# Streaming the columns of a matmul in another order, in nine stages of a two-block transformer kernel

## What is computed

```python
def swiglu(h, w_gu, w_down):                      # D_FF = 2816
    g, u = jnp.split(h @ w_gu, 2, axis=-1)
    return (jax.nn.silu(g) * u) @ w_down
...
    for i in range(DEPTH):                        # two layers, 272 tokens
        f = swiglu(rms_norm(h, ln_ffn1[i, 0]), ffn1_w_gu[i], ffn1_w_down[i])
        h = h + 0.5 * rms_norm(f, ln_ffn1[i, 1])
        # i == 0: a short convolution between two projections; i == 1: differential attention
        h = h + rms_norm(m, ln_mix[i, 1])
        f = swiglu(rms_norm(h, ln_ffn2[i, 0]), ffn2_w_gu[i], ffn2_w_down[i])
        h = h + 0.5 * rms_norm(f, ln_ffn2[i, 1])
    return h[:, N_META:]                          # 256 tokens from here on
...
    merged = (sigmoid(gate_a) * (o_a @ w_br_dsa) + sigmoid(gate_b) * (o_b @ w_br_moba))
    x = x + gt_m * (merged @ w_out)
    ...
    x = x + gt_f * ((jax.nn.silu(g_ff) * u_ff) @ w_down)
```

## Time and profile before

| | |
|---|---|
| median of 3 runs | 1584.47 us (1582.22 to 1591.33) |
| the profiled execution's own time | 1585.17 us |
| its span, first to last instruction | 1583.4 us |
| TensorE busy with matmuls | 1499.4 us, 11846 matmuls |
| weight loads busy | 1471.8 us |
| VectorE, ScalarE busy | 1059.7 us, 684.2 us |
| mean granted clock of TensorE | 0.969 |

### The profile page before, as it was taken

One profiled execution on the slowest core, in us unless ns is written; L12 is line 12 of the kernel. 1 busy time (PEld: TensorE's weight loads), 2 busy tenths in 40 slices (PEclk: granted clock), 3 DMA queues, 4 the chain that ended last, 5 costly groups with the idle time before them and its releaser, 6 DMA issues. The chain is left out here.

```text
span 1583.4 us, 28871 instructions
## 1 busy us (share of the span) xinstructions
PE 1499.4 (95%) x11846; PEld 1471.8 (93%) x11846; DVE 1059.7 (67%) x1416; ACT 684.2 (43%) x806; POOL 14.7 (1%) x31
## 2 busy tenths in 40 slices
PE   5999989989999899999899889999699999989999
PEld 5999989989999899999888689999688989989999
DVE  5666777776667766667766576667867665676653
ACT  5434353454433544433445364443432435454431
POOL 0000000000000000000000000000000000000000
PEclk9999999999999999999899799999799999999999
DMA  8455655435456654556332135547434224445450
GB/s 315 161 186 184 224 202 186 161 127 192 168 183 225 222 187 159 176 206 254 128 115 107 54 119 201 192 179 259 154 133 146 95 107 161 159 164 207 165 202 34
DMA packets 38156, 269.11 MB, mean 170 GB/s; under 512 B 4241, under 2 KB 5393, under 8 KB 5681
## 3 DMA queue, kind: packets, MB, share of 16 engines
q1 hardware_dynamic: 33120, 240.31, 42.0%
q0 software_dynamic: 3792, 26.44, 4.6%
q10 hardware_dynamic: 1152, 1.05, 0.2%
HBM read 266.73 MB, written 1.05 MB: 169 GB/s over the span
## 5 line engine op out<-in xcount | busy, mean ns | idle before, releaser
L328 PE MATMUL ps<-x_hi,w_hi 128*128 128x272 f32 (+1 forms) x2512 | 742.4, 296 | 44.2 <-DVE w_lo L865 15.6
L329 PE MATMUL ps<-x_lo,w_hi 128*128 128x272 f32 (+1 forms) x2512 | 728.4, 290 | 0.0
L330 PE MATMUL ps<-x_hi,w_lo 128*128 128x272 f32 (+1 forms) x2512 | 727.5, 290 | 0.0
L1601 ACT ACTIVATE w_hi<-raw_weights 128x2048 fp32r<-128x2048 f32 x228 | 434.9, 1911 | 385.0 <-PE ps L330 380.5
L865 DVE TENSOR_TENSOR w_lo<-raw_weights,w_hi 128x2048 fp32r<-128x2048 f32 x194 | 442.3, 2290 | 167.5 <-ACT w_hi L1601 167.1
L328 PEld LDWEIGHTS ps<-x_hi,w_hi 128*128 128x128 f32 x2512 | 486.5, 194 | 52.4 <-issue 29.6
L329 PEld LDWEIGHTS ps<-x_lo,w_hi 128*128 128x128 f32 x2512 | 486.6, 194 | 2.8 <-issue 2.4
L330 PEld LDWEIGHTS ps<-x_hi,w_lo 128*128 128x128 f32 x2512 | 485.6, 193 | 0.0
L328 PE MATMUL ps<-a_hi,w_hi 128*128 128x272 f32 (+1 forms) x1008 | 288.1, 286 | 1.5 <-DVE w_lo L865 1.3
L330 PE MATMUL ps<-a_hi,w_lo 128*128 128x272 f32 (+1 forms) x1008 | 287.5, 285 | 0.0
L329 PE MATMUL ps<-a_lo,w_hi 128*128 128x272 f32 (+1 forms) x1008 | 287.3, 285 | 0.0
(11 more groups left out here) (211 smaller groups left out, 1008.3 us busy)
## 6 DMA issues: line engine op xcount, KB each, us to landing
raw_weights<-w_units SPq DMA_DIRECT2D x228, 1024.0 KB, 4.8
mod_w<-mod_units POOLq DMA_DIRECT2D x24, 1024.0 KB, 5.1
h<-x_in SPq DMA_DIRECT2D x1, 1088.0 KB, 5.5
out<-h ACTq DMA_DIRECT2D x8, 128.0 KB, 1.8
con<-constants POOLq DMA_DIRECT2D x1, 592.0 KB, 8.4
tab<-tables POOLq DMA_DIRECT2D x1, 512.0 KB, 3.5
f<-constants POOLq DMA_DIRECT2D x1, 136.0 KB, 8.3
vec<-vectors SPq DMA_DIRECT2D x1, 100.5 KB, 2.0
```

Source lines behind the costliest of these rows:

```text
L328: pe.matmul(dst, wh, hi, start=start, stop=False)
L329: pe.matmul(dst, wh, lo, start=False, stop=False)
L330: return pe.matmul(dst, wl, hi, start=False, stop=stop)
L1601: act.activation(w_hi[:, u % RING, :], raw[:, u % RING, :], ACT.Copy).then_inc(S["hi_ready"], 1)
```

## The change

`three_pass` takes an optional pair (c, d). The row of T columns is then seen as c equal parts, and the stream takes d columns of the first part, d of the second, and so on, then the next d of each. Destination, high and low operand are rearranged alike, so that each column still lands in its own PSUM column. With (2, 8) and T = 272 a matmul reads 34 runs of 8 columns from halves that lie 136 columns apart; with (4, 4) and T = 272, 68 runs of 4 columns from quarters 68 apart; with (2, 16) and T = 256, 16 runs of 16 from halves 128 apart; with (4, 16) and T = 256, 16 runs of 16 from quarters 64 apart. The pair is looked up by the stage's key; stages without an entry stream as before. The number of instructions, their order on every engine, their waits, the weight loads and the number of columns of each matmul stay.

```diff
+ORDER = {("up", 1): (2, 8), ("down", 1): (2, 8), ("up", 2): (4, 4), ("down", 2): (4, 4),
+         ("up", 3): (2, 16), ("down", 3): (2, 16), ("up", 4): (4, 16), ("down", 4): (4, 16), "w_out": (4, 16)}
...
-            def three_pass(dst, slot, col, hi, lo, start, stop):
+            def three_pass(dst, slot, col, hi, lo, start, stop, order=None):
 
+                if order is not None:
+                    dst, hi, lo = (v.rearrange("p (c b d) -> p b c d", c=order[0], d=order[1]) for v in (dst, hi, lo))
                 wh, wl = w_hi[:, slot, col:col + P], w_lo[:, slot, col:col + P]
                 pe.matmul(dst, wh, hi, start=start, stop=False)
...
                             ins = three_pass(ps[:, st.bank(t), 0:st.T], u % RING, (kk * GROUP + m) * P,
-                                             xs[0][:, k, 0:st.T], xs[1][:, k, 0:st.T], k == 0, k == KT - 1)
+                                             xs[0][:, k, 0:st.T], xs[1][:, k, 0:st.T], k == 0, k == KT - 1,
+                                             ORDER.get(st.key))
...
                         ins = three_pass(ps[:, st.bank(st.t0 + m), 0:st.T], u % RING, (kk * 8 + m) * P,
-                                         xs[0][:, k, 0:st.T], xs[1][:, k, 0:st.T], k == 0, k == 2 * st.units - 1)
+                                         xs[0][:, k, 0:st.T], xs[1][:, k, 0:st.T], k == 0, k == 2 * st.units - 1,
+                                         ORDER.get(st.key))
```

More of the change, by code:

```diff
@@ L62, with __init__ @@
 C_ALL = C_MASK + TOK
+ORDER = {("up", 1): (2, 8), ("down", 1): (2, 8), ("up", 2): (4, 4), ("down", 2): (4, 4),
+         ("up", 3): (2, 16), ("down", 3): (2, 16), ("up", 4): (4, 16), ("down", 4): (4, 16), "w_out": (4, 16)}
 class Stage:
-    def __init__(self, plan, name, units, tiles, tokens, k_outer, quad_banks=False, tail=False):
+    def __init__(self, plan, key, name, units, tiles, tokens, k_outer, quad_banks=False, tail=False):
+        self.key = key
         self.name, self.units, self.tiles, self.T = name, units, tiles, tokens
@@ L121, in stage @@
         def stage(name, key, units, tiles, tokens, k_outer, quad=False):
-            stages[key] = Stage(plan, name, units, tiles, tokens, k_outer, quad,
+            stages[key] = Stage(plan, key, name, units, tiles, tokens, k_outer, quad,
                                 tail=k_outer and key not in ("br_dsa", "br_moba"))
```

## The result

The changed kernel is slower: 1595.22 us (median of 10 runs, 1594.36 to 1597.48) against 1584.2 us (10 runs), a ratio of 1.0063 with a 95% interval of 1.0052 to 1.0074 (the two medians divided give 1.0070). The forecast was 1566 us.

A forecast was written before the change was run, and what follows sets the result against it. TensorE's matmul step was taken as the bound. Minus 3 ns in nine stages summed to 12.7 + 3.2 + 0.2 + 1.6 + 0.6 = 18.3 us off 1585.17, less 0.7 for the median: 1566 us, range 1550 to 1620.

The forecast's parts named there:

- signs of being wrong: In the nine stages: four orders acting with different signs, or a step below the branches' 113.3 ns, would refute the prediction.
- (a): All nine stages: the moving stream, advancing slower, meets the weight stream less often; minus 3 ns a matmul.
- What was at stake: Nine stages' excess per matmul over undisturbed steps: 4.3 to 4.6 ns at 256 columns, 5.1 to 5.6 at 272.
- third rival, more meetings: Nine stages: a stream keeping the weights' pace may stay beside them; 20 us slower, 1604 us; chance 0.14.
- The sign that I had named for it: Weight loads in the trace after: more meetings would show as longer loads, 192 ns instead of 188.
- (b): Jumps between runs, 34, 68, 16 and 16 in a matmul: taken to cost nothing; rival at 0.42 ns each, 1675 us, chance 0.13.
- (c): Down 3: bound by VectorE's chain, TensorE waits 1.3 us for `w_lo`, so faster matmuls gain only 0.2 us there.
- The estimate of 120.0 ns for undisturbed 272 columns: Stages with 272 columns: the branches' 113.3 ns plus 6.7 for 16 columns more gives an undisturbed step of 120.0 ns.
- What I called steady inside gate/up 4: Gate/up 4, same shapes: eleven steps in a row of 120.0 ns and seven others of 112.9 ns.
- the comparison of the branches with `w_out`: Same code and 256 columns, 113.3 against 118.0 ns: the difference was put down to which addresses are read.

The follow-up runs named there:

- e5: Kernel before, old order, with all 128 weight columns in the nine stages read from a single column; 1578.32 us.
- e6: Changed kernel, new order, with all 128 weight columns in the nine stages read from a single column; 1591.61 us.
- e13: Against the kernel before, down 0 to 2 sweep, unit by unit, the distance between halves or quarters and an unbroken row's start, with 256 columns; 1599.98 us.
- e8: Kernel before, old order, with only the places where the moving rows of stages 3 and 4 begin changed; 1580.4 us.
- e11: Against the kernel before, other pairs in seven stages, such as (2, 8) in gate/up 3 and (2, 4) in down 3; 1604.31 us.
- e1: Changed kernel with only the PSUM destination rearranged and the moving operands read in the old order; 1588.33 us.
- e14: Kernel before with (17, 4) in all 272-column stages, (16, 4) in `w_in`, and rows 192 bytes after the weights' place in stages 3 and 4; 1556.80 us.
- e2: Changed kernel with only the moving operands rearranged and the destination written in the old order; 1596.93 us.
- e3: Changed kernel with the pairs of stages 1 and 2 exchanged, and those of stages 3 with stages 4 and `w_out`; 1596.76 us.
- e12: Changed kernel with only the halves kept, in stages 1 and 3, the other five stages in the old order; 1594.13 us, ratio 1.0060.
- e4: Changed kernel with other pairs, such as (2, 68) in stages 1, runs of 2 floats in stages 2 and eighths in stages 4; 1794.86 us.

## Why the prediction was wrong

The reading of the profile held. TensorE's step is the bound, the clock in the windows is 1.00 before and after, and 1 to 5 ns of a step decide the result. Where the four orders should each have taken 3 ns off, the two that read halves put 4.6 and 5.6 ns (272 columns) and 2.4 and 3.6 ns (256) on, and the quarters came to between minus 0.5 and plus 2.2. Different signs for the orders were among the signs of being wrong that I had named.

The step that failed is (a), "a reader that is not overtaken meets the other less often". It turned a picture of two readers into minus 3 ns a matmul without a row that showed the sign, and the halves measured plus 2.4 to 5.6. The picture is right in a part: with the weight stream held at one place the old order loses 2.4 ns of gate/up 3's step and its differences between rows (e5). But halves keep their price then (e6), and they keep it at every distance of the sweep (e13). What makes the price inside the reader stays open.

What was at stake was also tied to the wrong thing. The 4.3 ns between 113.3 and 117.6 are, at 256 columns, mostly the start of the row against the weights' place: the same unbroken order steps by 113.3, 117.8, 118.7 or 120.0 ns with the start (e8, e13). In the changed kernel gate/up 3 lost its good starts: the rows 192 bytes after went up by 4.4 ns, from 115.6 to 120.0, and the three other kinds of row by 1.7 to 1.9. The start is not all of it, since one start can have two steps (e8).

My third rival, more meetings, had the direction and twice the size (20 us, measured 11), and I gave it 0.14. The sign that I had named for it, weight loads of 192 ns instead of 188, did not come: 190 in gate/up 1, 188 in `w_out`. That halves need a moving weight stream to cost is refuted by e6.

(b) was right that there is no fixed price for a jump: quarters in runs of 4, with 64 runs in a matmul, step at two distances by the same 113.3 ns as the unbroken row from their start (e13). But it is not nothing for every order, and within halves the price grows with the number of jumps (e11). The strict sentence of the Trainium skill (Advanced Engine Details and Errata, PSUM Cachelines), that any non-contiguous pattern slows a matmul significantly, is not borne out for writing at runs of 4 to 16 floats: e1 has 125.7 and 117.6 ns in gate/up 1 and 3, beside 125.4 and 117.7. The 16-byte lines of the Trainium skill (SBUF — State Buffer, Door 1: The DMA port swizzle) agree with the runs of 2 floats, 239 ns against 125, but they are not the whole rule, since halves in whole lines cost.

(c) held in its mechanism: down 3 grew by only 0.4 us although 528 steps grew by 3.6 ns (1.9 us), since its wait for `w_lo` of 1.3 us disappeared. I had used it for a gain; it also takes up a loss. The gain side is in e8: at 113.4 ns a step down 3 waited 3.9 us for `w_lo` and, at a mean clock of 0.97, came out longer than before.

The estimate of 120.0 ns for undisturbed 272 columns was not reached; the best stage measured is 122.4. What I called steady inside gate/up 4 was: the start goes with 113.3 or 120.0 (e13, down 2). But the comparison of the branches with `w_out` was not one of addresses, for in other runs of the same places each took the other's step (e8, e1; in e14 both did).

Open: why two parts cost 6.7 to 10 ns where four parts in the same runs of 4, from the same start, cost 0 to 5.6 (e13); why some orders of eight parts cost too ((8, 4) 123.0 and 123.2, (8, 16) 121.2) and others hardly; and what chooses between 113.3 and 117.8 ns at one place. The loss of this change is shown to be made by the order of reading (e1, e2), by the pairs and not their place in the program (e3), and by the halves alone (e12). e6 rules out that it needs a moving weight stream. The distance matters where it is a multiple of 256 bytes (e4, e13) and does not explain the halves' price elsewhere. No run here looks into the reader itself.

## What to carry to other kernels

When a kernel is bound by back-to-back matmuls, compare the step between starts across stages of the same shape: a difference of 4% here hung on where and in what order the moving operand is read. The sign of such an effect has to be measured order by order, and an order has to be compared with the unbroken one from the same start. One stage can map many of them, since each unit can carry another arm (e13). In this kernel it paid to keep runs at whole groups of 4 floats, to try starts first and parts second, and to avoid two parts.

## What the runs showed of the hardware beside that

With 256 columns the same instruction stream steps by 113.3, 117.8, 118.7 or 120.0 ns a matmul, which goes with the start of the moving row, and stays there, for whole stages at the first three (e8) and for a unit at 120.0 (e13). From one start, 192 bytes after the weights' place, stages of the sixteen traces stood at 113.3 to 113.7 ns 21 times, at 117.8 to 118.0 twelve times and at 114.6 once. Quarters exactly 256 bytes apart in runs of 4 floats cost 136.1 ns, 272 bytes apart (272 columns) nothing. Runs of 2 floats cost 239 ns. After an added wait of 3.2 us at a stage's start the granted clock fell to its lower level for part of the following unit, with steps of 213 ns (e13, down 2).
